# Gate and up products of sixteen experts: one matmul of 128 columns, or four of 32 columns side by side

## What is computed

```
for e in range(N_EXPERTS):                                  # 16
    he = jax.nn.silu(t @ w1[e]) * (t @ w3[e])               # gate and up, 1024 -> 512
    y = y + combine[:, e:e + 1] * (he @ w2[e])              # down, 512 -> 1024
```

## Time and profile before

| what | value |
|---|---|
| median of 3 runs | 1277.82 us (1275.99 to 1280.12) |
| span of the profiled execution, first to last instruction | 1276.5 us |
| PE busy | 1234.5 us, 97% |
| PEld busy | 775.1 us, 61% |
| DVE, ACT, POOL busy | 46%, 18%, 29% |
| PE busy in gate and up (L2111) | 222.6 us |
| PE busy in down (L2130) | 112.6 us |
| mean granted TensorE clock | 0.992 |

### The profile page before, as it was taken

The page is one execution under the profiler, slowest core; times in us unless marked ns, Lnnn a source line. Parts: engine busy times, 40 slices in busy tenths (PEclk is TensorE's granted clock), DMA queues, the critical chain, the costliest instruction groups (busy, mean ns, idle before and its releaser), DMA issues.

```text
span 1276.5 us, 12824 instructions
## 1 busy us (share of the span) xinstructions
PE 1234.5 (97%) x4912; PEld 775.1 (61%) x4913; DVE 582.5 (46%) x1097; ACT 232.8 (18%) x482; POOL 370.3 (29%) x313
## 2 busy tenths in 40 slices
PE   4999999999999999999999999999899999999996
PEld 1567677777777777777777777555444444444442
DVE  2553378455766671663343354466422323132223
ACT  3221256123560001001100100112111011010100
POOL 0465500576002342343333330000312313222222
PEclk9899999999999999999999999999999999999998
DMA  9844220012201111111111154412997988888761
GB/s 353 291 175 156 74 75 1 17 66 75 75 1 65 68 67 66 66 66 66 66 66 66 66 214 165 165 66 103 379 422 297 366 319 362 336 336 354 304 238 34
DMA packets 59994, 209.07 MB, mean 164 GB/s; under 512 B 9568, under 2 KB 10144, under 8 KB 53792
## 3 DMA queue, kind: packets, MB, share of 16 engines
q1 hardware_dynamic: 47328, 186.25, 38.1%
q0 software_dynamic: 12288, 21.52, 4.7%
q10 hardware_dynamic: 320, 0.53, 0.1%
HBM read 208.24 MB, written 23.10 MB: 181 GB/s over the span
## 4 chain that ended last, share of the span: by engine, by line
PE 95%; DVE 2%; DMA 1%; ACT 0%; issue 0%; POOL 0%; SPq 0%; POOLq 0%; DVEq 0%
PE psum L1954 33%; PE psum L2111 17%; PE psum L1760 11%; PE psum L2130 9%; PE psum L2018 5%; PE psum L1738 4%; PE psum L1862 3%; PE psum L1680 3%; PE psum L1922 3%; PE psum L1896 1%; PE psum L2091 1%; DMA weight_ring<-in_w_ada 1%; PE psum L1775 1%; PE psum L2118 1%; PE psum L1902 1%; PE psum L2033 1%
## 5 line engine op out<-in xcount | busy, mean ns | idle before, releaser
L1954 PE MATMUL psum<-arena,weight_ring 128*128 128x320 f32 x928 | 256.9, 432 | 0.0
L2111 PE MATMUL psum<-weight_ring,arena 128*128 128x512 f32 x512 | 222.6, 592 | 0.3 <-ACT arena L1017 0.3
L1954 PEld LDWEIGHTS psum<-arena,weight_ring 128*128 128x128 f32 x928 | 175.9, 190 | 72.7
L638 POOL TENSOR_TENSOR weight_ring<-weight_ring 128x512 f32<-128x512 f32 x80 | 106.2, 1328 | 353.0 <-DMA weight_ring<-in_w_in 199.5
L1954 PE MATMUL psum<-x,weight_ring 128*128 128x320 f32 x640 | 179.5, 432 | 0.0
L2111 PEld LDWEIGHTS psum<-weight_ring,arena 128*128 128x128 f32 x512 | 96.1, 190 | 115.3 <-issue 114.7
L1954 PEld LDWEIGHTS psum<-x,weight_ring 128*128 128x128 f32 x640 | 121.1, 190 | 49.6
L2130 PE MATMUL psum<-arena 128*128 128x512 f32 x256 | 112.6, 593 | 0.7 <-ACT arena L1025 0.7
L639 POOL TENSOR_TENSOR weight_ring<-weight_ring 128x512 f32<-128x512 f32 x80 | 109.7, 1372 | 0.0
L1357 DVE TENSOR_TENSOR arena<-psum,arena 128x320 f32<-128x320 f32 x124 | 59.5, 488 | 92.3 <-PE psum L1954 91.8
L1622 DVE SCALAR_TENSOR_TENSOR arena<-psum,ropeC,arena 128x512 f32<-128x512 f32 x16 | 12.0, 751 | 188.5 <-ACT arena L1021 188.5
(11 more groups left out here) (268 smaller groups left out, 1335.3 us busy)
## 6 DMA issues: line engine op xcount, KB each, us to landing
weight_ring<-in_w SPq DMA_DIRECT2D x32, 2048.0 KB, 11.9
weight_ring<-in_w_in SPq DMA_DIRECT2D x16, 2048.0 KB, 8.1
arena<-in_w SPq DMA_DIRECT2D x16, 2048.0 KB, 11.9
arena<-in_w_ada SPq DMA_DIRECT2D x6, 2048.0 KB, 11.8
weight_ring<-in_w_ada SPq DMA_DIRECT2D x8, 1024.0 KB, 14.4
x<-in_x_sample SPq DMA_DIRECT2D x2, 2048.0 KB, 12.4
weight_ring<-in_w_conv_out SPq DMA_DIRECT2D x2, 2048.0 KB, 8.1
weight_ring<-in_w_attn_out SPq DMA_DIRECT2D x2, 2048.0 KB, 8.1
```

Source lines behind the costliest of these rows:

```text
L638: nc.gpsimd.tensor_tensor(out[:, 0:2], a_[:, 0:2], b_[:, 0:2], op)
L1954: last = mm(product_psum(q, name), w[:, k, :], src[:, k, :], start=(k == 0), stop=(k == 3))
L2111: last = mm(psum[:, 1024 + 512 * j:1536 + 512 * j], xgT[:, t, :], w[:, t, :], start=(t == 0), stop=(t == KT - 1))
```

## The change

The inner matmul of `gate_up` is split over the columns of its stationary operand. Each of the four lanes takes 32 tokens, writes 32 partitions of the same bank, and has the same slice of the weights as its moving operand.

```
--- before.py
+++ after.py
@@ -2108,7 +2108,9 @@
                         tr(late_rows_psum[0:16, 0:P], rowpack[:, 48:64], ident[:, :]).then_inc(s_late_packT, 1)
                     w = gu_slot[2 * b + j].rearrange("p (k n) -> p k n", k=KT)
                     for t in range(KT):
-                        last = mm(psum[:, 1024 + 512 * j:1536 + 512 * j], xgT[:, t, :], w[:, t, :], start=(t == 0), stop=(t == KT - 1))
+                        for lane in range(4):
+                            part = slice(32 * lane, 32 * (lane + 1))
+                            last = mm(psum[part, 1024 + 512 * j:1536 + 512 * j], xgT[:, t, part], w[:, t, :], start=(t == 0), stop=(t == KT - 1))
                 last.then_inc(s_gu, 1)
```

## The result

| | median | range | runs |
|---|---|---|---|
| before | 1278.05 us | 1275.93 to 1280.38 | 11 |
| changed | 1282.68 us | 1281.17 to 1286.14 | 11 |

The ratio is 1.0036, with a 95% interval of 1.0025 to 1.0046: 3.2 to 5.9 us slower. The forecast was 1282.5 us.

A forecast was written before the change was run, and what follows sets the result against it. PE was taken to bound the kernel. Splitting the 512 gate and up records adds 0 us, entering and leaving 17 narrow stretches 4.7 us: 1277.8 + 4.7 = 1282.5 us, range 1277 to 1306 us.

The forecast's parts named there:

- The bound: PE, busy for 97% of the span, never idle in gate and up; time added to PE there moves the end equally.
- 0 us per slot: Gate and up: each 429 ns record of 128 columns becomes four 32-column records running together, adding 0 us.
- The two-lane row: L1738, two lanes of 64 columns streaming the same weights: 32 records in 7.02 us, 219 ns a record.
- The bound of 5.6 us for the instructions: Gate and up: four load and matmul pairs at the transposes' 110 ns take 440 ns; at most 5.6 us more.
- The borders: Passing between 32-column matmuls and full-width work around them: 17 stretches at 0.275 us for entry and exit, 4.7 us.
- 0.155 in the stretch: Cost at a narrow stretch's first and last records, from L1738: 7.02 us where 6.86 us was expected.
- 0.12 in the transposes: Extra for transposes beside narrow stretches: four of L1775 take 0.59 us, four of L2118 between full-width pieces 0.47.
- The sum: Whole kernel: 0 us from the 512 gate and up records, 4.7 us from entries and exits, giving 1282.5 us.
- Not slower: Rival: entry and exit of a narrow stretch cost under 0.225 us, about 2.0 us in all, 1279.9 us; 17 in 100.
- Strict order, or two groups at most: Rival: at most two lanes run together in gate and up, by order or array feed: +222.6 us, 1500 us; 10 in 100.

## Why the prediction was right

- **The bound.** PE was hardly ever idle in the stage (the one wait of some size, for VectorE in the first expert, fell from 0.70 to 0.52 us and took up a little of the cost), and what was added to it moved the end: 0.34 us an expert makes 5.1 us from the first to the last gate and up matmul, and the medians differ by 4.6.
- **0 us per slot.** Held, from two lanes to four: 2048 records in 223.3 us, loads in fours 0.43 us apart. The two-lane row was the right neighbour. The bound of 5.6 us for the instructions was not needed; two lanes and four cost the same.
- **The borders.** The mechanism held (a border twice per expert costs twice as much, for an eighth of the split matmuls and for one and a half times as many); the term was sized a little small. Forecast 0.275 us for an entry and exit: 0.155 in the stretch and 0.12 in the transposes. Measured 0.34 to 0.35: 0.14 or 0.15 in the stretch, 0.11 + 0.09 in the transposes. The stretch was right and the transposes too cheap. The 0.12 set four transposes of L1775 against four of L2118, which are not the same kind. Set against themselves in the trace before, four of L1775 take 0.44 us between full-width work, 0.50 behind a narrow stretch, and 0.59 between two:

```profile
70.09 0.60 PE L1775 MATMUL psum<-ident,arena 128*128 128x128 f32 x4
70.53 1.89 PE L1760 MATMUL psum<-weight_ring,x 128*128 128x256 f32 x8
...
91.85 0.66 PE L1775 MATMUL psum<-ident,arena 128*128 128x128 f32 x4
92.35 0.60 PE L1692 MATMUL psum<-ident,arena 128*128 128x128 f32 x4
```

  So leaving costs 0.06 us there and entering 0.09. Entering costs 0.09 in gate and up as well; leaving costs 0.11, 0.05 more. The first load behind a narrow stretch is no longer hidden (before, it began 0.43 us ahead of the transposes; after, with them), and the loads of L2091 are 52 ns longer than those of L1775:

```profile
1051.21 0.19 PEld L2091 LDWEIGHTS psum<-ident,arena 128*128 128x128 f32 x1 [0.24 <-issue]
...
1052.44 0.96 PEld L2091 LDWEIGHTS psum<-ident,arena 128*128 128x128 f32 x8 [0.84 <-issue]
...
L2091 PEld LDWEIGHTS psum<-ident,arena 128*128 128x128 f32 x128 | 15.4, 193 | 12.9 <-issue 12.9
...
L1775 PEld LDWEIGHTS psum<-ident,arena 128*128 128x128 f32 x80 | 9.7, 141 | 4.9 <-issue 3.2
```

  (The first line is of before, the next two of after, the last is the same in both.) That the 52 ns are the missing 0.05 us fits the numbers; no run tests it.
- **The sum.** 0.29 us for the divided first expert (16.57 us for 16.28 up to the next gate and up) and 15 x 0.35 make some 5.5 us where I had 4.7; the interval, 3.2 to 5.9 us, holds both. The close hit of the median owes something to luck.
- **"Not slower"** needed borders under 0.225 us; they are 0.34.
- **Strict order, or two groups at most.** By the Trainium skill, "TensorE: Matmul & The Clock Gate" (section on packing small matmuls), matmuls stay in program order; four lanes would then have cost 222 us. The traces disagree with that: the stretch takes 13.88 us, and 13.94 with four records of each lane in a row; a lane starts past three records that wait in the lane before it, and only a longer run of one lane holds the others back. I gave this 10 in 100 because no row went beyond two lanes. The runs of four and eight steps a lane show that a large loss is close by, at another order of the same loops.

## What to carry to other kernels

Splitting a matmul that already fills the array's columns gained nothing here: its time is that of the stream. Lanes pay where columns stand empty and each lane can have a stream of its own, as in the modulation products (10.5 us, 0.8%). Count how often TensorE passes between full-width and narrow work, not how much of it is narrow, and change the lane with every step or two, never after long runs.

## What the runs showed that I had not expected

- By the three runs on the order, a lane of the array takes a running record of an f32 matmul and three waiting ones, and the next one for that lane stops the queue for all lanes. Two steps a lane (4 records) cost 0.06 us a stretch, four steps (8 records) 15.9, eight steps (16 records) 29.4.
- A weight load at f32 takes 110 ns for 32 columns, 137 for 64 (L2113 with two lanes) and 190 for 128. Four of them overlap to 0.13 us.

```profile
L2113 PEld LDWEIGHTS psum<-weight_ring,arena x1024: 132/137/138, 909.8 to 1252.1; 128*64 128x64 f32 x171
```

- Where TensorE waits anyway, the granted clock can take back what less work gives: in the first 42 us it was 0.89 with five products in four lanes and 0.97 with six, which have the same products there, and 1.00 with three. It differs between executions, so that less work lowers it isn't shown.
